# Applying a norm's root behind the matrix products instead of ahead of them, in a fused two-block fp32 kernel

## The chip, the cores and the metric

One core of a Trainium2 chip runs the whole program. The metric is device time in microseconds, the median of three runs. PE is the tensor engine, DVE the vector engine, ACT the scalar engine, POOL the GpSimd engine and SP the queue that loads the weights.

## What is computed

Two transformer blocks on 512 tokens with width 1024, in fp32. The first block (gated linear recurrence, convolution, a PEER layer with 16384 experts) ends in a norm, the second one has an attention with dilated windows, an MLP, a differential attention, an MLP, and a last norm. What matters here is the tail:

```python
def rms_norm(x, g):
    y = x * lax.rsqrt(jnp.mean(x * x, axis=-1, keepdims=True) + EPS)
    return y * g

h = h + g2 * peer_layer(...)
h = rms_norm(h, final_g)                           # norm 2
h = h + attention_a(rms_norm(h, mix_g[0]))         # norm 3
h = h + sq_relu_mlp(rms_norm(h, mlp_g[0]), ...)    # norm 4
h = h + attention_b(rms_norm(h, mix_g[1]))         # norm 5
h = h + sq_relu_mlp(rms_norm(h, mlp_g[1]), ...)    # norm 6
return rms_norm(h, final_g_2)                      # norm 7

def sq_relu_mlp(xn, w_in, w_out):
    h = jax.nn.relu(xn @ w_in)
    return (h * h) @ w_out
```

## The kernel before, in words

The activations stay in SBUF, transposed: hT holds h as eight tiles of 128 features by 512 tokens. Weights come as 568 panels of 128 outputs by 1024 inputs, in one fixed order, through a ring of four slots (SP). A panel is an fp32 product made of three fast ones: the weights are split into a high part (ACT, high_w, line 772) and a low part (POOL, ring_r, line 1874), the activations into a high part (for the norms uT_r, in the MLPs and attention outputs the tiles `parts`) and a low part (sq_r), and PE adds high by high, high by low and low by high, 24 matmuls of 512 columns for a panel (lines 350 to 352). Each panel goes into one of four PSUM banks, and PE may write a bank again when `bank_free` says that it has been read. ACT prepares panel j+3 when panel j is done, so weights are ready two panels ahead.

A norm r runs like this. While the eight panels of the projection before it finish, DVE adds each into hT (`residual`, lines 1593 and 1596), ACT squares the tile into sq (line 792) and PE sums the squares over the partitions with a matmul against ones, two panels later (`behind`, `square_sum`, line 388; an fp32 matmul, which the trace lists as two). After the last panel, `norm` does the last two sums. DVE makes the mean (line 1312), ACT the rough reciprocal root (line 780), DVE one Newton step of three instructions (lines 1305 to 1307). Then DVE scales all eight tiles by weight and root (`scaled`, line 1322), ACT copies their high parts into uT_r (line 820), DVE subtracts to get the low parts in sq_r (line 1334), and only then may PE begin the next panels.

Norm 2's output is itself h (its `scaled` writes hT), and norm 3 squares that again, so these two run one behind the other with no product between them. Norms 3 and 5 feed 24 panels of q, k and v each, which ACT copies out of PSUM (lines 1120, 1122, 1126); the value tiles are then transposed by PE and copied by ACT (line 1114). Norms 4 and 6 feed the MLPs: in groups of eight hidden tiles ACT applies Relu out of PSUM into one of four buffers `gel` (line 1055), DVE squares the tile (line 1673) and splits it (lines 1317, 1318). The order is up(0), then up(g+1), down(g) in turn. All engines meet by semaphores alone; each engine's order is its program text.

## Time and profile before

| | us |
|---|---|
| median of 3 runs (lowest, highest) | 4031.61 (4026.58, 4033.82) |
| the profiled execution's own time | 4038.15 |
| its span, first to last instruction | 4036.3 |
| mean granted TensorE clock | 0.967 of full |
| PE busy | 3796.2 (94%) |
| DVE, ACT, POOL busy | 2159.3, 1339.2, 1370.9 |

Line numbers are those of the kernel before. In the timeline an entry says when an instruction started, how long it ran, and in brackets how long its engine had been idle and who released it. Matmuls overlap, so the distance between starts counts, not their length.

### The profile page before, as it was taken

What the parts mean: (1) busy time and instruction counts of PE and PEld (TensorE: products, weight loads), DVE (VectorE), ACT (ScalarE), POOL (GpSimd) and SP (SyncE); (2) the same over time, 40 slices, a digit from 0 to 9 for tenths busy, and PEclk for the clock granted to TensorE, in tenths of its full rate; (3) what the DMA queues carried; (4) which work ended last, traced back from release to release, by engine and by line L of the source; (5) the groups of instructions that cost most, each with busy time, mean ns of one, the idle gap of its engine ahead of it and who ended that gap; (6) DMA issues with size and microseconds to landing.
All of it is one profiled execution on the core that took longest, in us unless ns stands there. A gap on an engine that the chain in (4) does not pass through costs nothing.

```text
span 4036.3 us, 49951 instructions
## 1 busy us (share of the span) xinstructions
PE 3796.2 (94%) x17036; PEld 2977.2 (74%) x17036; DVE 2159.3 (53%) x3575; ACT 1339.2 (33%) x1852; POOL 1370.9 (34%) x588
## 2 busy tenths in 40 slices
PE   7998997899999999979999999999899989988998
PEld 4888785678888888858888886754588868357886
DVE  3776897507576676237777774125363320546441
ACT  3444322223434344311111112346322233653221
POOL 1122242333343333334444443320144434223442
PEclk8999998999999999989999999989999999999999
DMA  4334321223364554666666652221122222212222
GB/s 171 131 108 147 129 94 53 79 94 110 110 208 136 182 160 158 207 196 183 198 187 182 182 182 86 79 74 46 42 94 95 94 74 96 68 41 82 95 94 78
DMA packets 266639, 486.55 MB, mean 121 GB/s; under 512 B 16721, under 2 KB 148177, under 8 KB 266097
## 3 DMA queue, kind: packets, MB, share of 16 engines
q1 hardware_dynamic: 81936, 299.93, 23.6%
q10 hardware_dynamic: 184580, 184.95, 14.1%
q8 instruction: 81, 1.33, 0.1%
q14 instruction: 42, 0.34, 0.0%
HBM read 415.48 MB, written 84.02 MB: 124 GB/s over the span
## 4 chain that ended last, share of the span: by engine, by line
PE 51%; issue 34%; POOL 11%; DVE 2%; ACT 2%; POOLq 0%; DMA 0%; DVEq 0%; ACTq 0%
PE ps L350 15%; PE ps L352 14%; PE ps L351 14%; POOL ring_r L1874 11%; PE ps L655 3%; PE ps L673 2%; PE ps L663 1%; PE ps L388 1%; DVE sq L1322 1%; ACT arena L1142 0%; PE ps L691 0%; DVE arena L1726 0%; ACT L1177 0%; ACT L1175 0%; ACT high_w L772 0%
## 5 line engine op out<-in xcount | busy, mean ns | idle before, releaser
L1874 POOL TENSOR_TENSOR ring_r<-ring,high_w 128x1024 fp32r<-128x1024 f32 x552 | 1345.1, 2438 | 2495.8 <-ACT high_w L772 1931.5
L350 PE MATMUL ps<-uT_r,high_w 128*128 128x512 f32 x2752 | 1105.4, 402 | 97.5 <-POOL ring_r L1874 40.0
L352 PE MATMUL ps<-uT_r,ring_r 128*128 128x512 f32 x2752 | 1082.3, 393 | 0.0
L772 ACT ACTIVATE high_w<-ring 128x1024 fp32r<-128x1024 f32 x424 | 446.7, 1056 | 1090.7 <-PE ps L352 938.5
L351 PE MATMUL ps<-sq_r,high_w 128*128 128x512 f32 x2048 | 803.5, 392 | 0.0
L351 PE MATMUL ps<-part,high_w 128*128 128x512 f32 x1856 | 735.4, 396 | 0.0
L350 PEld LDWEIGHTS ps<-uT_r,high_w 128*128 128x128 f32 x2752 | 524.7, 191 | 221.3 <-issue 82.8
L350 PE MATMUL ps<-part,high_w 128*128 128x512 f32 x1536 | 613.6, 399 | 4.9 <-POOL ring_r L1874 4.9
L352 PE MATMUL ps<-part,ring_r 128*128 128x512 f32 x1536 | 607.4, 395 | 0.0
L352 PEld LDWEIGHTS ps<-uT_r,ring_r 128*128 128x128 f32 x2752 | 522.9, 190 | 112.1
L351 PEld LDWEIGHTS ps<-sq_r,high_w 128*128 128x128 f32 x2048 | 389.2, 190 | 78.6
L351 PEld LDWEIGHTS ps<-part,high_w 128*128 128x128 f32 x1856 | 350.3, 189 | 89.7 <-issue 7.4
L350 PEld LDWEIGHTS ps<-part,high_w 128*128 128x128 f32 x1536 | 288.9, 188 | 78.2 <-POOL ring_r L1874 5.4
L352 PEld LDWEIGHTS ps<-part,ring_r 128*128 128x128 f32 x1536 | 288.7, 188 | 70.1
L1726 DVE CUSTOM_DVE_ANT_0 arena<-ps,arena 128x512 f32<-128x512 f32 x128 | 87.7, 690 | 392.9 <-PE ps L655 234.8
L1317 DVE TENSOR_SCALAR part<-arena 128x512 fp32r<-128x512 f32 x192 | 292.5, 1523 | 6.6
L1318 DVE TENSOR_TENSOR part<-arena,part 128x512 fp32r<-128x512 f32 x192 | 274.1, 1427 | 6.6
L1596 DVE TENSOR_TENSOR hT<-ps,hT 128x512 f32<-128x512 f32 x80 | 55.4, 692 | 380.4 <-PE ps L352 380.4
L1673 DVE TENSOR_TENSOR arena<-arena 128x512 f32<-128x512 f32 x192 | 134.3, 699 | 226.3 <-ACT arena L1055 117.5
L1000 ACT ACTIVATE act_out<-ps 128x512 f32<-128x512 f32 x128 | 76.5, 598 | 492.1 <-PE ps L352 380.7
L1593 DVE SCALAR_TENSOR_TENSOR hT<-ps,ada,hT 128x512 f32<-128x512 f32 x136 | 102.1, 751 | 234.1 <-PE ps L352 234.1
L1659 DVE TENSOR_TENSOR st<-cst,ps 128x512 f32<-128x512 f32 x128 | 87.6, 684 | 206.2 <-PE ps L582 180.6
(275 smaller groups left out, 4015.1 us busy)
## 6 DMA issues: line engine op xcount, KB each, us to landing
ring<-panels SPq DMA_DIRECT2D x568, 512.0 KB, 3.5
adram<-act_out ACTq DMA_DIRECT2D x128, 256.0 KB, 3.9
gdram<-arena ACTq DMA_DIRECT2D x16, 2048.0 KB, 10.3
arena<-gdram ACTq DMA_DIRECT2D x128, 256.0 KB, 5.4
arena<-adram ACTq DMA_DIRECT2D x128, 256.0 KB, 2.7
arena<-ada_rest ACTq DMA_DIRECT2D x32, 512.0 KB, 4.2
strips_dram<-btab ACTq DMA_DIRECT2D x4, 3584.0 KB
arena<-strips_dram ACTq DMA_DIRECT2D x32, 448.0 KB, 3.3
```

Of the source, the lines that this page charges most:

```text
L350: t_.matmul(out, wh, xh, start=(k == 0), stop=False)
L351: t_.matmul(out, wh, xl, start=False, stop=False)
L352: last = t_.matmul(out, wl, xh, start=False, stop=(k == KT - 1))
L655: t_.matmul(ps[:, qt, :], qs[64 * hh:64 * hh + 64, par, qt * P:(qt + 1) * P], ks[64 * hh:64 * hh + 64, par, :], start=True, stop=True).the ...
L772: s_.activation(high_w[:, j % RING], ring[:, j % RING], ACT.Copy).then_inc(hi_ready, 1)
L1317: S.done(v_.tensor_scalar(high, src, 1.0, None, ALU.mult))
L1318: return v_.tensor_tensor(low, src, high, ALU.subtract)
L1593: ins = v_.scalar_tensor_tensor(out=hT[:, j, :], in0=ps[:, j % BANKS, :], scalar=ada[:, gain + j:gain + j + 1], in1=hT[:, j, :], op0=ALU.m ...
L1659: S.mark(v_.tensor_tensor(arng[:, four, :], keys, of_slots(0), ALU.is_equal))
L1673: S.done(v_.tensor_tensor(gel[:, j % 4, :], gel[:, j % 4, :], other, ALU.mult))
L1726: v_.tensor_tensor_reduce(out=pb[:, par, hh, qt, :], in0=ps[:, qt, :], in1=strip[:, hh, P * (3 - qt):P * (3 - qt) + T], scale=1.0, scalar= ...
L1874: g_.tensor_tensor(ring_r[:, j], ring[:, j], high_w[:, j], ALU.subtract).then_inc(lo_ready, 1)
```

## The change

Norms 3 to 6 no longer scale the activations by the root. The panels run on h times the norm's weight (for norm 3 the product of the weights of norms 2 and 3), which ACT and DVE split tile by tile as each residual tile gets ready (`high_of`, `low_of`), and the root of each token multiplies the panel's result: DVE, not ACT, takes q, k and v out of PSUM and multiplies by rstd; in the MLPs DVE multiplies the relu by rstd before it squares it. PE starts panel 0 and does the last two square sums behind it. Squares go to a ring of three tiles in st instead of sq, with a new semaphore `sq_used`. The two norms that adjoin become one pass: ACT squares both h and h times final_g, PE sums both (banks 4 and 5), and `norms_2_3` makes one root from the other; hT is scaled by norm 2's weight and root while the k panels run. The split attention output moves from uT_r to kT_r (parts[1]), because uT_r is now written while the output projection runs. Norms 0, 1 and 7 stay. The diff, without its smaller pieces:

```diff
             def square_sum(r, k):
-                if k == 0 and r:
+                if k == 0:
                     pe.wait_ge(rs_ms, RS_NORM[r])
-                pe.wait_ge(sq_ready, KT * r + k + 1)
-                ins = t_.matmul(ps[:, 4, :], ones[:], sq[:, k, :], start=(k == 0), stop=(k == KT - 1))
+                if r == 2:
+                    for n in range(2):
+                        pe.wait_ge(sq_ready, KT * r + 2 * k + n + 1)
+                        ins = t_.matmul(ps[:, 4 + n, :], ones[:], st[:, 1 + (2 * k + n) % 3, :], start=(k == 0), stop=(k == KT - 1))
+                        ins.then_inc(stat_done if k == KT - 1 else sq_used, 1)
+                    return
+                pe.wait_ge(sq_ready, KT * (r + (r > 2) - (r > 3)) + k + 1)
+                src = st[:, 1 + k % 3, :] if r in FOLDED else sq[:, k, :]
+                ins = t_.matmul(ps[:, 4, :], ones[:], src, start=(k == 0), stop=(k == KT - 1))
                 if k == KT - 1:
                     ins.then_inc(stat_done, 1)
+                elif r in FOLDED:
+                    ins.then_inc(sq_used, 1)
             def behind(r, j):
                     square_sum(r, j - 2)
             def norm(r):
-                for k in range(0 if r in (0, 3) else KT - 2, KT):
+                for k in range(KT - 2, KT):
...
+            def up(q, r=None):
                 for j in range(8):
-                    panel(q, j, (uT_r, sq_r), ready=None if j else ready)
+                    panel(q, j, (uT_r, sq_r), ready=normed(r) if r and j == 0 else None)
+                    if r and j == 0:
+                        norm(r)
...
-                norm(r)
                 for j in range(16):
                     panel(q_qkv + j // 8, j % 8, (uT_r, sq_r), ready=None if j else normed(r))
+                    if j == 0:
+                        norm(2 if s == 0 else 5)
...
-                    panel(q_wo, j, (uT_r, qT_r), ready=None if j else (a["oT_ready"], 0))
+                    panel(q_wo, j, (kT_r, qT_r), ready=None if j else (a["oT_ready"], 0))
...
+                if r == 2:
+                    for n in range(2):
+                        m = 2 * k + n
+                        if m >= 3:
+                            act.wait_ge(sq_used, m - 2)
+                        s_.activation(st[:, 1 + m % 3, :], hT[:, k, :], ACT.Square, scale=col("final", k) if n else 1.0)\
+                          .then_inc(sq_ready, 1)
+                    return
+                if r in FOLDED and k >= 3:
+                    act.wait_ge(sq_used, FOLDED[r] - 2 + k - 2)
+                s_.activation(st[:, 1 + k % 3, :] if r in FOLDED else sq[:, k, :], hT[:, k, :], ACT.Square).then_inc(sq_ready, 1)
+
+            GAIN = {4: "mlp0", 5: "mix1", 6: "mlp1"}
+
+            def high_of(r, k):
+
+                residual_done(2 if r == 3 else r, k)
+                s_.activation(uT_r[:, k, :], hT[:, k, :], ACT.Copy, scale=small[:, 64 + k:65 + k] if r == 3 else col(GAIN[r], k))\
+                  .then_inc(x_high, 1)
...
+                        if r in (2, 4, 5, 6):
+                            high_of(3 if r == 2 else r, j - 1)
                         square(r, j - 1)
+                if r in (2, 4, 5, 6):
+                    high_of(3 if r == 2 else r, KT - 1)
+                    square(r, KT - 1)
...
+                    if first and j == 1:
+                        root(RS_NORM[4 if s == 1 else 6], 5 if s == 1 else 7)
...
-                    if j < 8:
-                        ins = s_.activation(qT[:, j, :], ps[:, j % BANKS, :], ACT.Copy, scale=-0.125)
...
                     high(q_qkv, j + 3)
+                    if j == 0:
+                        root(RS_NORM[2 if s == 0 else 5], 3 if s == 0 else 6)
+                    if j == 1 and s == 0:
+                        root(RS_NORM[3], 4)
...
+            def low_of(r, k):
+
+                ve.wait_ge(x_high, KT * SPLIT_NORM[r] + k + 1)
+                v_.scalar_tensor_tensor(out=sq_r[:, k, :], in0=hT[:, k, :],
+                                        scalar=small[:, 64 + k:65 + k] if r == 3 else col(GAIN[r], k), in1=uT_r[:, k, :],
+                                        op0=ALU.mult, op1=ALU.subtract).then_inc(u_ready, 1)
+
+            def residuals(q, gain, r=None):
+
+                for j in range(8):
+                    residual(q, j, gain)
+                    if r in FOLDED and j:
+                        low_of(r, j - 1)
+                if r in FOLDED:
+                    low_of(r, 7)
+
+            def norms_2_3():
+
+                ve.wait_ge(stat_done, RS_NORM[3] + 1)
+                rsqrt(RS_NORM[2], D, out=sr)
+                S.done(v_.tensor_tensor(ms[:], sr[:], sr[:], ALU.mult))
+                S.done(v_.scalar_tensor_tensor(out=ms[:], in0=ps[:, 5, :], scalar=1.0 / D, in1=ms[:], op0=ALU.mult, op1=ALU.mult))
+                v_.tensor_scalar(ms[:], ms[:], EPS, None, ALU.add).then_inc(rs_ms, 1)
+                newton(RS_NORM[3])
+                S.done(v_.tensor_tensor(rstd[:], rstd[:], sr[:], ALU.mult))
...
+                if s:
+                    S.done(v_.tensor_tensor(gel[:, j % 4, :], gel[:, j % 4, :], rstd[:], ALU.mult))
                 S.done(v_.tensor_tensor(gel[:, j % 4, :], gel[:, j % 4, :], other, ALU.mult))
...
-                down(s, e + 2)
+                down(s, e + 2, 5 if s == 1 else None)
...
+                if s:
+                    rsqrt(RS_NORM[5], D)
+                for j in range(24):
+                    taken(q_qkv, j)
+                    bank = ps[:, j % BANKS, :]
+                    if j < 8:
+                        ins = v_.scalar_tensor_tensor(out=qT[:, j, :], in0=bank, scalar=-0.125, in1=rstd[:], op0=ALU.mult, op1=ALU.mult)
+                    elif j < 16:
+                        ins = v_.tensor_tensor(kT[:, j - 8, :], bank, rstd[:], ALU.mult)
+                    else:
+                        if j >= 18:
+                            ve.wait_ge(vt_done, 8 * s + j - 17)
+                        ins = v_.tensor_tensor(vf[:, j % 2, :], bank, rstd[:], ALU.mult)
+                    ins.then_inc(bank_free[j % BANKS], 1)
+                    if s == 0 and j == 7:
+                        for k in range(KT):
+                            S.mark(v_.scalar_tensor_tensor(out=hT[:, k, :], in0=hT[:, k, :], scalar=col("final", k), in1=sr[:],
+                                                           op0=ALU.mult, op1=ALU.mult))
+                        S.wait()
...
-            for j in range(KT):
-                residual(Q_WO_A, j)
-            norm(4, lambda k: col("mlp0", k))
+            attention(0, Q_QKV_A)
+            residuals(Q_WO_A, None, 4)
+            rsqrt(RS_NORM[4], D)
             hidden(1, Q_MLP_A, 4)
```

## Rows read from the trace of the kernel before

**Rows 1.** The page: instruction count and busy time of each engine.

```profile
span 4036.3 us, 49951 instructions
PE 3796.2 (94%) x17036; PEld 2977.2 (74%) x17036; DVE 2159.3 (53%) x3575; ACT 1339.2 (33%) x1852; POOL 1370.9 (34%) x588
```

**Rows 2.** Waits of PE from 2505 us on (engine, line, releaser: total, times, longest).

```profile
PE ps L350 <- DVE sq_r L1334: 39.3, 4, 9.9
PE ps L388 <- ACT sq L792: 9.4, 6, 5.3
PE ps L691 <- issue: 5.0, 1, 5.0
```

**Rows 3.** Timeline, norms 2 and 3 (start us, length, engine line; [idle before <-releaser]).

```profile
2504.73 0.75 DVE L1593 SCALAR_TENSOR_TENSOR hT<-ps,ada,hT 128x512 f32<-128x512 f32 x1 [5.70 <-PE ps L352]
2512.00 5.39 DVE L1322 SCALAR_TENSOR_TENSOR hT<-hT,cc,st 128x512 f32<-128x512 f32 x8
2523.61 0.69 DVE L1312 TENSOR_SCALAR st<-ps 128x512 f32<-128x512 f32 x1 [6.21 <-PE ps L388]
2524.39 0.63 ACT L780 ACTIVATE st<-st 128x512 f32<-128x512 f32 x1 [6.24 <-DVE st L1312]
2525.05 0.69 DVE L1305 SCALAR_TENSOR_TENSOR st<-st 128x512 f32<-128x512 f32 x1 [0.76 <-ACT st L780]
2527.24 5.39 DVE L1322 SCALAR_TENSOR_TENSOR sq<-hT,cc,st 128x512 f32<-128x512 f32 x8
2532.54 4.90 DVE L1334 TENSOR_TENSOR sq_r<-sq,uT_r 128x512 fp32r<-128x512 f32 x8
2540.57 0.60 ACT L1120 ACTIVATE arena<-ps 128x512 f32<-128x512 f32 x1 [7.28 <-PE ps L352]
```

**Rows 4.** Four stretches, last panel's end to next panel's end (us; busy; clock; DMA).

```profile
2504.73:2540.57 35.84, 19.94 (x47) 10.55 (x46) 21.89 (x33) 14.98 (x25) 2.35 (x1) 0.76 0.05 15
2910.02:2931.76 21.74, 11.13 (x31) 7.38 (x30) 13.66 (x21) 9.25 (x14) 2.35 (x1) 0.76 0.08 26
3283.84:3307.04 23.20, 11.61 (x31) 7.42 (x30) 14.19 (x23) 10.73 (x16) 2.35 (x1) 0.71 0.07 23
3644.27:3665.83 21.56, 10.95 (x31) 7.25 (x30) 13.66 (x21) 9.25 (x15) 2.35 (x1) 0.76 0.08 24
```

**Rows 5.** Timeline of ACT in the first up-projections after norm 4.

```profile
2931.76 0.60 ACT L1055 ACTIVATE arena<-ps 128x512 f32<-128x512 f32 x1 [8.41 <-PE ps L352]
2937.20 0.60 ACT L1055 ACTIVATE arena<-ps 128x512 f32<-128x512 f32 x1 [3.89 <-PE ps L352]
```

**Rows 6.** Timeline of DVE in two output projections: panel ends without and with a square sum.

```profile
3600.79 0.69 DVE L1596 TENSOR_TENSOR hT<-ps,hT 128x512 f32<-128x512 f32 x1 [3.05 <-PE ps L352]
3606.39 0.69 DVE L1596 TENSOR_TENSOR hT<-ps,hT 128x512 f32<-128x512 f32 x1 [4.91 <-PE ps L352]
...
2903.57 0.69 DVE L1596 TENSOR_TENSOR hT<-ps,hT 128x512 f32<-128x512 f32 x1 [5.76 <-PE ps L352]
2910.02 0.69 DVE L1596 TENSOR_TENSOR hT<-ps,hT 128x512 f32<-128x512 f32 x1 [5.76 <-PE ps L352]
```

**Rows 7.** Timeline of DVE and POOL in one hidden tile of the first MLP.

```profile
2937.83 0.69 DVE L1673 TENSOR_TENSOR arena<-arena 128x512 f32<-128x512 f32 x1 [1.49 <-ACT arena L1055]
2938.56 0.43 DVE L1317 TENSOR_SCALAR part<-arena 128x512 fp32r<-128x512 f32 x1
2938.83 2.41 POOL L1874 TENSOR_TENSOR ring_r<-ring,high_w 128x1024 fp32r<-128x1024 f32 x1 [3.03 <-ACT high_w L772]
2939.02 2.76 DVE L1318 TENSOR_TENSOR part<-arena,part 128x512 fp32r<-128x512 f32 x1
```

**Rows 8.** Timeline of ACT and POOL where the qkv panels of the second attention end.

```profile
3435.04 0.60 ACT L1126 ACTIVATE arena<-ps 128x512 f32<-128x512 f32 x1 [3.89 <-PE ps L352]
3435.54 1.05 ACT L772 ACTIVATE high_w<-ring 128x1024 fp32r<-128x1024 f32 x1
3436.66 2.34 POOL L1874 TENSOR_TENSOR ring_r<-ring,high_w 128x1024 fp32r<-128x1024 f32 x1 [3.53 <-ACT high_w L772]
```

More of the change, by code:

```diff
@@ L70 @@
 SPLIT_NORM = {0: 0, 1: 1, 3: 2, 4: 3, 5: 4, 6: 5}
+FOLDED = {3: 0, 4: 16, 5: 23, 6: 30}
 class Steps:
@@ L233, in build @@
         qT, kT = (view(4096 * n, KT, T) for n in range(2))
-        qT_r = parts[0]
+        qT_r, kT_r = parts[:2]
         vtok = view(8192, TT, D)
@@ L604, in hidden @@
             def hidden(s, q8, groups):
-                up(q8, normed(4 if s == 1 else 6))
+                up(q8, 4 if s == 1 else 6)
                 with pe.Fori(0, groups // 2 - 1) as i:
@@ L800, in last_before @@
                     if j:
+                        if r in (2, 4, 5, 6):
+                            high_of(3 if r == 2 else r, j - 1)
                         square(r, j - 1)
+                if r in (2, 4, 5, 6):
+                    high_of(3 if r == 2 else r, KT - 1)
+                    square(r, KT - 1)
             def norm(r):
-                for k in range(0 if r in (0, 3) else KT - 1, KT):
+                for k in range(0 if r == 0 else KT - 1, KT):
                     square(r, k)
                 root(RS_NORM[r], r + (r >= 1))
-                if r in SPLIT_NORM and r:
+                if r == 1:
                     high_x(r)
@@ L1105, in _ @@
             last_before(2, Q_PEER + 31)
-            norm(2)
             def attention(s, r, q_qkv):
                 a = att[s]
-                norm(r)
                 def token_major(j):
@@ L1181, in high_b @@
                     act.wait_ge(b_out, u + 1)
-                    s_.activation(uT_r[:, u, :], act_out[:, 0, :], ACT.Copy).then_inc(b_high, 1)
+                    s_.activation(kT_r[:, u, :], act_out[:, 0, :], ACT.Copy).then_inc(b_high, 1)
                 def round_b(n):
@@ L1259, in attention @@
                         act.wait_ge(weighed, k + 1)
-                        s_.activation(uT_r[:, k, :], qT[:, k, :], ACT.Copy).then_inc(o_high, 1)
+                        s_.activation(kT_r[:, k, :], qT[:, k, :], ACT.Copy).then_inc(o_high, 1)
                 else:
@@ L1273, in _ @@
             last_before(4, Q_WO_A)
-            norm(4)
             hidden(1, Q_MLP_A, 4)
@@ L1280, in _ @@
             last_before(6, Q_WO_B)
-            norm(6)
             hidden(2, Q_MLP_B, 4)
@@ L1320, in scaled @@
             def scaled(r, k, gain):
-                v_.scalar_tensor_tensor(out=(hT if r == 2 else sq)[:, k, :], in0=hT[:, k, :], scalar=gain(k),
+                v_.scalar_tensor_tensor(out=sq[:, k, :], in0=hT[:, k, :], scalar=gain(k),
                                         in1=rstd[:], op0=ALU.mult, op1=ALU.mult).then_inc(upre if r in SPLIT_NORM else u_ready, 1)
@@ L1366, in gain_of @@
             def gain_of(r):
+                if r == 1:
+                    S.done(v_.tensor_tensor(small[:, 64:72], cc[:, COLS["final"]:COLS["final"] + 8], cc[:, COLS["mix0"]:COLS["mix0"] + 8],
+                                            ALU.mult))
                 name = "norm1" if r == 0 else "norm2"
@@ L1679, in up, with down @@
                     tile(s, g, j, par)
-            def down(s, q):
-                for j in range(8):
-                    residual(q, j, 40 if s == 0 else None)
+            def down(s, q, r=None):
+                residuals(q, 40 if s == 0 else None, r)
             def hidden(s, q8, groups):
                 up(s, q8, 0, 0)
-                with S.loop(groups // 2 - 1, 32) as i:
+                with S.loop(groups // 2 - 1, 48 if s else 32) as i:
                     up(s, i * 4 + (q8 + 1), i * 2 + 1, 1)
@@ L1709, in _, with attention @@
                 stored_down(i * 2 + (q + 2), i * 2 + 2, 0)
-            down(0, q + GROUPS - 1)
-            norm(2, lambda k: col("final", k))
-            def attention(s, r):
+            down(0, q + GROUPS - 1, 3)
+            norms_2_3()
+            def attention(s, q_qkv):
                 a = att[s]
-                norm(r, lambda k: col("mix0" if s == 0 else "mix1", k))
+                if s:
[7 more added lines that the diff above has]
+                        ins = v_.tensor_tensor(kT[:, j - 8, :], bank, rstd[:], ALU.mult)
+                    else:
+                        if j >= 18:
[7 more added lines that the diff above has]
+                        S.wait()
                 def strip_wait(n, hh):
@@ L1849, in _ @@
             S.done(v_.tensor_scalar(lamc[:, 3:4], lamc[:, 2:3], -LAMBDA_INIT, None, ALU.add))
-            attention(1, 5)
-            for j in range(KT):
-                residual(Q_WO_B, j)
-            norm(6, lambda k: col("mlp1", k))
+            attention(1, Q_QKV_B)
+            residuals(Q_WO_B, None, 6)
+            rsqrt(RS_NORM[6], D)
             hidden(2, Q_MLP_B, 4)
@@ L1908, in low_b @@
                 po.wait_ge(b_high, u + 1)
-                g_.tensor_tensor(qT_r[:, u, :], act_out[:, 0, :], uT_r[:, u, :], ALU.subtract).then_inc(a["oT_ready"], 1)
+                g_.tensor_tensor(qT_r[:, u, :], act_out[:, 0, :], kT_r[:, u, :], ALU.subtract).then_inc(a["oT_ready"], 1)
             at_b = 8 * (Q_WO_B - Q_HEADS) // RING
```

59 lines of the change are left out of this document (20 added, 39 removed).

## The prediction, made before the changed kernel ran

> **What bounds the kernel now.** I read the page first: PE is busy 94% of the span, DVE 53%, ACT 33%, POOL 34% [rows 1]. So time is gained only where PE stands still, or where it does work that can be left out. Next I asked for the waits of PE from 2505 us on, the part that the change touches. The largest is four waits, 39.3 us together, of the first matmul of a panel for the low part of the activations; then 9.4 us in six waits of the square sums for ACT [rows 2]. Everything else listed there belongs to attention and is 5 us or less. The four are norms 3, 4, 5 and 6. The timeline of the first shows the chain: the last residual tile at 2504.73, eight scalings to hT from 2512.00, the second mean at 2523.61, eight more scalings, eight subtractions, and only at 2540.57 is the first new panel out of PE [rows 3]. That wait is listed as 9.9 us at most, because the square sums in the middle cut it, so the list of waits understates what a norm costs. The right measure is from the end of the last old panel to the end of the first new one. Those four stretches are 35.84, 21.74, 23.20 and 21.56 us, 102.34 us in sum, with the granted clock at 0.76, 0.76, 0.71 and 0.76 of full [rows 4]. Part of the time PE had the lower of its two levels, 1.2 instead of 2.4 GHz, so that the first panel behind the standstill is slow as well; that is inside these lengths.
>
> **What the stretches become.** A panel on (uT_r, sq_r) that waits for nothing takes 5.44 us (2937.20 less 2931.76) [rows 5]. One square sum costs PE 0.85 us: panels of an output projection end 5.60 us apart without one and 6.45 us with one [rows 6].
>
> Norms 4, 5 and 6. After the last old panel come the sum of tile 5 (0.85), panel 0 (5.44), then the sums of tiles 6 and 7, which now lie behind panel 0 (1.70). Together 7.99 us each, 24.0 us for three. They take 66.50 us now. Saved: 42.5 us.
>
> Norms 2 and 3. Each tile has two sums. After the last panel: two sums of tile 5 (1.70), panel 0 (5.44), four sums (3.40), 10.5 us. The five tiles summed behind earlier panels get one more each, 4.25 us. 14.8 us in place of 35.84. Saved: 21.0 us. The count is the same 16 sums as before: eight of them stood in the gap and now stand between panels, and can't be hidden. That is why the double norm gives less than its length promises.
>
> Sum 63.5 us. One sum might wait: the last square of norm 2/3 needs a slot of the ring of three, freed by the first of the four sums. That is 0.85 us after panel 0 ends; the square takes about 0.6, and PE has two more sums (1.7 us) before it asks for it. Nothing.
>
> **Is the new work hidden?** (a) Low parts at panel 0. Count from the end T of the last panel. ACT does high_w (1.05 us [rows 8]), then high part 6, square 6 and high part 7 at up to 0.60 us each, the length of its copies in rows 5: done by T+2.8. The timeline has DVE's subtraction, with both inputs in SBUF, take 2.76 us where it meets POOL's 2.41 us weight subtraction, though POOL began 0.19 us before it; the same form without POOL takes about 0.6 (eight in 4.90) [rows 3, 7]. It ended 0.54 us after POOL did. So DVE's low parts 6 and 7 may be held until POOL ends at about T+3.6, and be done at T+4.2 and T+4.8. Panel 0 starts at about T+0.7, asks for tile 6 after 18 of its 24 matmuls (T+4.8) and for tile 7 three later (T+5.5). It just fits: cost zero, bound above 0.7 us for each of four norms if either is one instruction later.
>
> (b) The root must exist when PE wants bank 0 again, at panel 4 (qkv), 3 x 5.44 = 16.3 us after the sums end. For norm 5: mean, ACT's root, three Newton instructions and one read, about 5 us. For norms 2/3 the chain is twice that: two means, two roots, six Newton instructions, a square, a product, an addition of EPS and a last product, at 0.72 us from one Newton step to the next (2525.05 to the scaling at 2527.24 are three) and 0.63 us per root [rows 3] about 10.5 us. The second root also stands in ACT behind taken(1) and a high_w, at about 6.6 us after the sums. So first read at 11.1 us, with 5.2 us to spare. In the MLPs the reader is ACT's relu, which does not need the root at all; four buffers `gel` give another four panels. Cost zero.
>
> (c) The extra product in the MLPs, 64 of 0.69 us, 44 us of DVE. Before, a tile takes 4.0 us from the relu (2937.83 to 2941.78) out of 5.44 [rows 7]. After: products until 1.4 us, then the copy of the high part meets POOL instead of the subtraction, is released at about 3.4, and the tile ends at about 4.5. Below 5.44, so PE stays the bound. When DVE is late at the start of an MLP (by some 5 us, the root), it must catch up: it needs 2.6 us of each 5.44, and POOL leaves it 3.0.
>
> (d) q, k, v out of PSUM by DVE: 48 times 0.69 instead of ACT's 0.60, on an engine that sat idle there. The eight scalings of hT (5.4 us) lie behind k panels with four banks between. Zero. ACT now begins the last high_w 0.5 us earlier (3435.04 instead of 3435.54), and POOL, which stages the second attention only after its last subtraction, follows [rows 8]; PE waits for both, in the first attention for ACT. I take 0.9 us off for the two, less 0.2 for DVE's slower copy.
>
> (e) The output projection reads kT_r instead of uT_r: the trace has two pitches for a panel without sums, 5.44 and 5.60 us [rows 5, 6], and these 16 panels already have the longer one. The tile's place might decide which, so the bounds are 16 x 0.16 = 2.6 us less or as much more; I take zero.
>
> The sum is 64.2 us, against the profiled execution's own 4038.15 us: 3973.9. The median of the runs is 4031.61, 6.5 lower, so I take the same gain from it: 3967.4 us.
>
> A rule that speaks against this change is in the Trainium skill, SBUF — State Buffer, "The single rule": DVE instructions with two SBUF inputs and GpSimd instructions that read SBUF lock each other out whole. By that rule the low parts, the Newton steps and the product by the root can all be held, which the trace shows for the subtraction alone. In norms 2/3 it holds two steps of the chain for up to 2.4 us each; first read would come at 15.9 instead of 11.1 us, still ahead of 16.3, so by it the sum stays at 3967.4.
>
> **The rivals.** *Part of the gap stays.* The margins of (a) are half a microsecond and of (b), all holds counted, half a microsecond too. If low parts are late in every norm at one POOL length (2.4 us) and the double chain overshoots by 3, 12.6 us are lost: 3980. For it: DVE is held for a whole POOL instruction in every hidden tile. Against: the margins as counted include that hold. Chance 0.2.
>
> *DVE becomes the bound of the up-projections (slower).* Place: `tile`, once the four `gel` buffers are used up. It decides from 5.44 us a tile. If both the new product and the copy or subtraction were held for a whole POOL instruction, a tile would take 4.0 + 2.77 = 6.7 us; 64 x 1.3 = 83 us, more than the 64 gained, so some 4050. Against it: POOL runs one 2.41 us instruction per panel and can't hold DVE twice in one, and down panels leave time to catch up. Chance 0.02.
>
> *The gaps were not what ends last.* If PE, freed of them, waited for weights instead (ACT and POOL must keep the pace through the norm), the time would be 4031. Against: in all panels away from norms ACT waits 3.9 us per panel for PE [rows 5], so they have room. Chance 0.02.
>
> *More than counted,* some 6 us more (3961): attention starts earlier in other ways, fewer holds. Chance 0.06.
>
> **How the numbers follow.** The forecast has 0.70, its own spread some 5 us either way (the runs of before spread by 7). The range goes from 3958, for the rival that gains more, to 3984, for the gap that stays in part. A measurement of this kernel can tell about 0.2%, 8 us, from no change; both of the main cases are far beyond that: faster 0.96, same 0.02, slower 0.02.
>
> **What would show it.** The wait of L350 for the low parts in norms 3 to 6 (39.3 us) falls to under 2. The four stretches become 10 to 11 us and three times 8, at full clock. PE busy hardly changes; DVE's rises by 44 us from the products and 33 from the PSUM reads, less the 32 scalings left out. PE shows no wait on ACT's relu or DVE's tile in the MLPs, and none for bank 0 at the fifth q panel. I am wrong if a wait for the new PSUM read appears there, if panel 0 stops at its seventh tile, or if up panels come more than 5.5 us apart.

## The result, and the profile after

The changed kernel takes 3968.36 us (median of 4 runs, 3962.99 to 3969.05), the kernel before 4030.86 beside it (4026.58 to 4033.82). The ratio is 0.9843, 95% interval 0.9826 to 0.986: faster by 1.57%, 62.5 us. The forecast was 3967.4, in a range of 3958 to 3984. Run once more with later experiments, the changed kernel came to 3961.81 and the same ratio, 0.9842 (0.9826 to 0.9859).

The profiled executions are 4038.15 us before and 3962.99 after, which is 75.2 apart. Segment by segment, below, 61.5 us of that can be put down to a cause or a place that repeats; the rest lies where executions of one kernel differ as well.

First the page after, instructions and busy time of each engine, to be held against [rows 1]:

```profile
span 3961.2 us, 50054 instructions
PE 3769.2 (95%) x17036; PEld 2968.6 (75%) x17036; DVE 2267.1 (57%) x3659; ACT 1315.1 (33%) x1804; POOL 1388.0 (35%) x588
```

PE has the same 17036 matmuls. DVE is up by 107.8 us and 84 instructions, ACT down by 24.1 us and 48 instructions, PE down by 27.0 us. The waits of PE from 2500 us on (engine, line, releaser: total, times, longest) answer to [rows 2]:

```profile
PE ps L675 <- ACT arena L1176: 6.4, 7, 1.7
PE ps L703 <- issue: 4.8, 1, 4.8
PE ps L351 <- DVE part L1900: 3.8, 4, 2.3
PE ps L351 <- POOL part L1979: 3.5, 1, 3.5
```

The 39.3 us for `sq_r` are gone from the list, and so are the 9.4 us for squares. What leads it now all belongs to attention. L351 waits there for the low part of the heads' output, as before.

The timeline of DVE from the last residual of the peer layer on, with lines left out, answers to [rows 3]:

```profile
2501.12 0.75 DVE L1646 SCALAR_TENSOR_TENSOR hT<-ps,ada,hT 128x512 f32<-128x512 f32 x1 [3.20 <-PE ps L353]
2502.82 3.04 DVE L1364 SCALAR_TENSOR_TENSOR sq_r<-hT,small,uT_r 128x512 fp32r<-128x512 f32 x2 [0.95 <-ACT uT_r L819]
2511.76 0.69 DVE L1338 TENSOR_SCALAR st<-ps 128x512 f32<-128x512 f32 x1 [5.90 <-PE ps L391]
...
2519.07 2.24 DVE L1331 SCALAR_TENSOR_TENSOR st<-st 128x512 f32<-128x512 f32 x1 [1.80 <-ACT st L790]
...
2523.53 1.89 DVE L1775 SCALAR_TENSOR_TENSOR arena<-ps,st 128x512 f32<-128x512 f32 x3
```

The last residual is followed at once by the two low parts, together 3.04 us, over at T+4.74. The first of them took 2.38 us instead of 0.75 beside GpSimd's weight subtraction (below, "held" is short for this). The double root is made beside panels 1 to 3. Its first use is at 2523.53, where three finished panels lie waiting, so three reads run back to back.

Three windows after (start:end length, PE, PEld, DVE, ACT, POOL busy, clock, DMA share and GB/s): the double norm, from the last residual up to the last of its sums; norm 4, up to the end of panel 0; the first MLP from last residual to last residual. The first two stand where [rows 4] had 35.84 and 21.74 us:

```profile
2501.12:2511.79 10.67, 10.67 (x37) 6.79 (x36) 3.81 (x4) 6.52 (x9) 3.25 (x2) 1.00 0.31 100
2881.14:2887.50 6.36, 6.36 (x27) 4.88 (x26) 3.74 (x3) 3.33 (x6) 2.41 (x1) 1.00 0.26 84
2881.14:3241.34 360.20, 360.20 (x1553) 291.32 (x1552) 186.76 (x172) 94.59 (x116) 162.23 (x64) 1.00 0.28 94
```

In all of them PE is busy the whole length, at full clock. The stretch of norm 4 is a standstill no more. The same MLP before, also from last residual to last residual:

```profile
2910.02:3283.84 373.82, 363.21 (x1553) 293.10 (x1552) 159.40 (x148) 94.74 (x116) 153.78 (x64) 0.99 0.28 90
```

The same 1553 matmuls took 363.21 us of PE; they now take 360.20. So of the 13.6 us gained, 10.6 was standing still and 3.0 was matmuls at the lower clock behind the standstill.

Divided at last residuals and at the reads of the last v panels, the whole second half compares as follows (us; each boundary is the start of an instruction in the timeline; before, the last v panels are read at 2668.58 and, as in [rows 8], at 3435.04):

| segment | before | after | difference | forecast |
|---|---|---|---|---|
| last peer residual to last v panel (norms 2 and 3) | 163.85 | 138.68 | -25.17 | -25.3 |
| attention A | 198.08 | 197.90 | -0.2 | -0.7 in both together |
| output projection A | 43.36 | 43.44 | +0.1 | 0 |
| MLP A (norm 4) | 373.82 | 360.20 | -13.62 | -13.75 |
| to last v panel (norm 5) | 151.20 | 136.15 | -15.05 | -15.21 |
| attention B | 165.75 | 160.15 | -5.6 | |
| output projection B | 43.48 | 44.94 | +1.5 | 0 |
| MLP B (norm 6) | 373.64 | 360.20 | -13.44 | -13.57 |
| tail (norm 7) | 18.4 | 18.4 | 0 | 0 |

The forecast of the first segment is 35.84 less 10.54; the 4.25 us for sums behind earlier panels lie ahead of that boundary. Of the 75.2 us, the four norm segments are 67.3. Less those 4.25 and the 1.5 of output projection B, 61.5 us are left, and the medians are 62.5 apart. The profiled executions of the changed kernel and its variants show what is chance in the rest: where they don't change an MLP or the tail they repeat it to 0.1 us, but attention A took between 190.2 and 197.9 us, attention B between 160.1 and 166.8, and the last peer residual came between 2499 and 2512 us in kernels with the same front. The traces of the changed kernel and of the one before have the granted clock at 0.91 in attention A, 0.96 in attention B of the changed kernel and 0.97 ahead of 2500 us. The 5.6 us of attention B, and the part ahead of 2500 us (3.6 us shorter though it holds 4.25 more), are within that spread, so nothing is read from them.

### The profile page after: what moved, and what is told of

The parts are those of the page before. It is cut to its first block, busy times and chain, and to the rows that moved or that the text cites. A ratio compares the mean times of both kernels' runs of the same rounds, so it can differ in the third digit from the quotient of the medians.

```text
span 3961.2 us, 50054 instructions
## 1 busy us (share of the span) xinstructions
PE 3769.2 (95%) x17036; PEld 2968.6 (75%) x17036; DVE 2267.1 (57%) x3659; ACT 1315.1 (33%) x1804; POOL 1388.0 (35%) x588
## 4 chain that ended last, share of the span: by engine, by line
PE 51%; issue 35%; POOL 11%; ACT 1%; DVE 1%; POOLq 0%; DMA 0%; DVEq 0%; ACTq 0%
PE ps L351 15%; PE ps L353 15%; PE ps L352 15%; POOL ring_r L1944 11%; PE ps L667 3%; PE ps L685 2%; PE ps L675 1%; PE ps L396 1%; PE ps L391 0%; ACT arena L1170 0%; DVE arena L1798 0%; PE ps L703 0%; ACT L1205 0%; ACT L1203 0%; POOLq L1943 0%
## 5 line engine op out<-in xcount | busy, mean ns | idle before, releaser
L351 PE MATMUL ps<-uT_r,high_w 128*128 128x512 f32 x2624 | 1046.9, 399 | 49.8 <-POOL ring_r L1944 38.5
L353 PE MATMUL ps<-uT_r,ring_r 128*128 128x512 f32 x2624 | 1027.1, 391 | 0.0
L352 PE MATMUL ps<-part,high_w 128*128 128x512 f32 x1856 | 735.3, 396 | 0.0
L351 PE MATMUL ps<-part,high_w 128*128 128x512 f32 x1664 | 669.5, 402 | 12.1 <-POOL ring_r L1944 4.8
L353 PE MATMUL ps<-part,ring_r 128*128 128x512 f32 x1664 | 658.6, 396 | 0.0
L351 PEld LDWEIGHTS ps<-uT_r,high_w 128*128 128x128 f32 x2624 | 496.9, 189 | 161.0 <-issue 36.8
L353 PEld LDWEIGHTS ps<-uT_r,ring_r 128*128 128x128 f32 x2624 | 495.7, 189 | 105.1
L1343 DVE TENSOR_SCALAR part<-arena 128x512 fp32r<-128x512 f32 x192 | 419.4, 2185 | 6.6
L352 PEld LDWEIGHTS ps<-part,high_w 128*128 128x128 f32 x1856 | 351.2, 189 | 88.6 <-issue 7.4
L351 PEld LDWEIGHTS ps<-part,high_w 128*128 128x128 f32 x1664 | 314.1, 189 | 94.2 <-issue 8.4
L353 PEld LDWEIGHTS ps<-part,ring_r 128*128 128x128 f32 x1664 | 314.3, 189 | 74.5
L352 PE MATMUL ps<-part_x,high_w 128*128 128x512 f32 x448 | 177.4, 396 | 0.0
```

The costliest lines, as they stand in the source:

```text
L351: t_.matmul(out, wh, xh, start=(k == 0), stop=False)
L352: t_.matmul(out, wh, xl, start=False, stop=False)
L353: last = t_.matmul(out, wl, xh, start=False, stop=(k == KT - 1))
L1343: S.done(v_.tensor_scalar(high, src, 1.0, None, ALU.mult))
```

## The experiments

**The last sums ahead of panel 0 or behind it.** The change puts the last two square sums (four in the double norm) behind the first new panel. Here they stand ahead of it again; all else is folded.

```diff
+                    if r and j == 0:
+                        norm(r)
                     panel(q, j, (uT_r, sq_r), ready=normed(r) if r and j == 0 else None)
-                    if r and j == 0:
-                        norm(r)
```

The same is done in attention.

> The changed kernel, but PE does the last two square sums (tiles 6 and 7) of norms 3 to 6 ahead of panel 0 instead of behind it. Theory (PE's order matters, the squares are not ready when the last panel ends): square 7 is written about 3.4 us after the last panel, so panel 0 starts some 1.8 us later in norms 4, 5, 6 and 0.9 us later in norms 2/3; in sum about 6 us slower than the changed kernel, and a wait of PE for ACT's squares of 5 to 7 us comes back. Rival (the order is indifferent, because PE would wait for the low parts at panel 0 anyway): within 1.5 us of the changed kernel.

Measured: 3969.92 us, ratio to before 0.9862 (0.9846 to 0.9879). The time alone doesn't settle it, but the segments do: 0.80 for the double norm and 1.88 each for norms 4, 5 and 6, 6.4 us in all, where about 6 was expected. PE's waits for squares are back with 4.3 us in three of them; 5 to 7 was expected. Nearly all of the gain is therefore the fold itself; the order of the sums is a tenth of it.

**What a square sum costs.** Each sum of the double norm is done a second time, into a bank that nobody reads.

```diff
                         pe.wait_ge(sq_ready, KT * r + 2 * k + n + 1)
+                        t_.matmul(ps[:, 6 + n, :], ones[:], st[:, 1 + (2 * k + n) % 3, :], start=(k == 0), stop=(k == KT - 1))
                         ins = t_.matmul(ps[:, 4 + n, :], ones[:], st[:, 1 + (2 * k + n) % 3, :], start=(k == 0), stop=(k == KT - 1))
```

> The changed kernel with each of the 16 square sums of norms 2/3 done twice (the copy goes to a bank that nobody reads). Theory (square sums between panels lie bare on PE, 0.85 us each): 13.6 us slower. Rival (PE has slack there, or only the four behind panel 0 count): 0 to 3.4 us slower.

Measured: 3977.18 us, ratio 0.9881 (0.9864 to 0.9897). The medians, 8.8 us apart from different sets of runs, can't settle 13.6; the segments can. The six extra sums behind the last residual make the first segment 143.82 instead of 138.68: 5.14, or 0.857 each. The down panels ahead of it come 9.02 us apart instead of 7.30, five times 1.72. That is 13.7 us in all. Each sum lies wholly on the path, on either side of the last panel.

**How full VectorE is.** A product like the new one is done once more, and in another kernel three times more, in each hidden tile of both MLPs; nobody reads it. The edit with one:

```diff
                 if s:
+                    for _ in range(1):
+                        S.done(v_.tensor_tensor(act_out[:, 0, :], gel[:, j % 4, :], rstd[:], ALU.mult))
                     S.done(v_.tensor_tensor(gel[:, j % 4, :], gel[:, j % 4, :], rstd[:], ALU.mult))
```

> The changed kernel with one more DVE product in each of the 64 hidden tiles, written to an unused buffer. Theory (PE is the bound, DVE's tile may be longer than a panel for a while because four buffers and the down panels absorb it): a tile then takes 5.8 us against 5.44 us a panel, lag of some 11 us after 16 tiles, no stall: within 2 us. Rival (the extra product has put DVE at the edge): 64 times 0.36 to 0.7 us, 23 to 45 us slower.

> The changed kernel with three more DVE products in each hidden tile. DVE needs about 7.2 us a tile with POOL's subtraction holding it once. Theory (only the first 16 tiles in a row can run DVE out of buffers): 10 to 30 us slower in all, PE waiting near the end of the second up group of each MLP and at the start of the first down group. Rival (DVE bound from the first tile on): 64 times 1.8, 115 us slower.

One more costs nothing: 3967.12 us, ratio 0.9852 (0.9835 to 0.9869), both MLPs 360.20 as without it. Three more cost 25.5 and 26.0 us in the MLPs, and 4017.15 in all (0.9972, 0.9962 to 0.9983), which gives back most of the gain. Between 10 and 30 was expected, and the two MLPs alone are 51.5: the price of running out of buffers was set too low, though the place was right. The windows of the first MLP with one more, and then of a stretch of three in the kernel with three more:

```profile
2886.01:3246.21 360.20, 360.20 (x1553) 291.35 (x1552) 211.36 (x204) 94.69 (x115) 164.65 (x64) 1.00 0.28 94
```

```profile
2985.00:3000.04 15.04, 0.86 (x4) 0.40 (x3) 14.49 (x21) 1.06 (x1) 2.34 (x1) 0.68 0.10 35
3000.04:3005.04 5.00, 5.00 (x14) 3.97 (x15) 1.65 (x3) 0.00 (x0) 0.00 (x0) 0.61 0.01 3
3005.04:3015.00 9.96, 9.96 (x45) 8.07 (x44) 1.38 (x2) 2.12 (x2) 2.99 (x2) 1.00 0.21 61
```

The stall has its place: not in the up panels, which have four banks and four `gel` tiles, but behind them. VectorE still works on tiles when the first down panels are finished, their residuals come late, and PE wants their banks (wait of 14.19 us for `hT`, DVE busy 14.49 of 15.04 us). Then PE runs at a clock of 0.61 for some 5 us. The three waits for `hT` in that MLP are 14.19, 2.08 and 2.08, 18.4 us, and two for the weights' low part add 1.4. The rest of its 25.5 is PE's busy time, 365.95 us for the same 1553 matmuls instead of 360.20.

**One fold alone.** Norm 4 is put back as before (sums in one go, scale, high part, low part, no root in the tiles of MLP A). The other three stay folded.

```diff
-FOLDED = {3: 0, 4: 16, 5: 23, 6: 30}
+FOLDED = {3: 0, 5: 16, 6: 23}
...
-            rsqrt(RS_NORM[4], D)
+            norm(4, lambda k: col("mlp0", k))
...
-                if s:
+                if s == 2:
                     S.done(v_.tensor_tensor(gel[:, j % 4, :], gel[:, j % 4, :], rstd[:], ALU.mult))
```

> Norm 4, between the first output projection and the first MLP, is put back as it was: sums in one go ahead of the products, h scaled by the root and the weight, then split, and no root in that MLP's tiles. The other three stay folded. Theory (each fold is worth its own gap and nothing else moves): the first MLP from last residual to last residual goes from 360.20 back to 373.82, the second stays at 360.20, the norms 2 and 3 gap stays at 10.7; whole time 13.6 us above the changed kernel. Rival (the folds gain from each other, by the clock or by the weight transfers that a gap let run ahead): the difference is under 9 or over 18 us, or another segment moves by over 1 us.

Measured: 3978.76 us against 3961.81 of the changed kernel on the same chip; ratios to before 0.9881 (0.9865 to 0.9896) and 0.9842. The difference of medians, 17.0 us, is blurred by attention. MLP A takes 372.67, MLP B stays at 360.20 and the first segment at 138.67: the fold is worth 12.5 us, and no other segment outside attention moves by over 0.4 us. That is 1.1 less than expected, since this gap came out shorter than before's, 20.59 us to the relu of panel 0 instead of 21.74; why is open. The wait is back alone, in the list of waits of this kernel, and its window has the low clock, 0.75 where [rows 4] has 0.76:

```profile
PE ps L351 <- DVE sq_r L1359: 9.8, 1, 9.8
```

```profile
2877.93:2898.52 20.59, 9.98 (x31) 6.54 (x30) 13.66 (x21) 9.26 (x14) 2.35 (x1) 0.75 0.08 27
```

**How much room the double root has.** Ten products that nobody reads are put into its chain, each waited for.

```diff
                 rsqrt(RS_NORM[2], D, out=sr)
+                for _ in range(10):
+                    S.done(v_.tensor_tensor(act_out[:, 0, :], sr[:], sr[:], ALU.mult))
```

> Ten more products of 128x512 stand in the chain of the roots of norms 2 and 3, each waited for, which nobody reads. By the theory the chain is off the path with slack: its first read of a panel comes 12.2 us after the last residual's sums and the bank is needed at 15.9, so 3.7 us are free. At 0.69 to 0.72 us each the ten are 7.0 us: the first attention segment (last residual of the peer layer to last v panel) grows by 3.3 us, 138.7 to 142, more if some are held by GpSimd at 2.4 (each hold adds 1.7), and nothing else moves: +3 to +7 in all. Rival (the chain is on the path already, its whole length counts): +7 or more with no hold. Second rival (later work has slack that takes it all up): +0.

Measured: 3976.37 us, ratio 0.9871 (0.9856 to 0.9886). The first segment is 147.92, 9.2 us longer, and none of the others outside attention changes by over 0.1 us. 3.3 was expected without holds, and 3 to 7 with them. 9.2 is outside that and inside the bounds of the first rival, which says 7 or more if the whole chain is on the path; so the time alone doesn't decide, and the timeline has to. In the medians it is 14.6 us (3961.81 to 3976.37), with attention's spread in it. Lines of the timelines of DVE and PE in this kernel:

```profile
2519.06 0.69 DVE L1338 TENSOR_SCALAR st<-ps 128x512 f32<-128x512 f32 x1 [5.89 <-PE ps L391]
...
2522.69 9.30 DVE L1382 TENSOR_TENSOR act_out<-st 128x512 f32<-128x512 f32 x10
...
2536.11 2.72 DVE L1333 SCALAR_TENSOR_TENSOR st<-st 128x512 f32<-128x512 f32 x1
2538.86 2.71 DVE L1387 TENSOR_TENSOR st<-st 128x512 f32<-128x512 f32 x1
2541.60 2.49 DVE L1777 SCALAR_TENSOR_TENSOR arena<-ps,st 128x512 f32<-128x512 f32 x4
```

```profile
2542.44 0.77 PE L351 MATMUL ps<-uT_r,high_w 128*128 128x512 f32 x1 [7.08 <-DVE arena L1777]
```

From the start of the first mean to the first read are 22.54 us here and 11.77 without the ten, so the chain became 10.8 longer, not 7.0. The ten took 9.30 us rather than about 7.2, because one of them was held (2.77), and two later steps were held at 2.7; without the ten only one step was (2.24). PE waits 7.08. The room is thus 10.8 less 7.1, 3.7 us, as stated: had the whole chain been on the path, as the rival has it, PE would have waited all of the 10.8. The other 2 us are PE's own: nine matmuls behind the wait begin 0.43 us apart instead of 0.23, at the lower clock. So the theory of the room holds, and the price of overstepping it was set too low.

**The sums on VectorE.** The second experiment says that a square sum on PE is never hidden, the third that VectorE has room. So VectorE adds up the squares (one copy, seven additions), and PE keeps one product with ones per mean, behind panel 0. ScalarE makes high part and square ahead of its next weight part.

```diff
+            def add_square(r, k):
...
+                    src = st[:, 1 + m % 3, :]
+                    if k:
+                        ve.wait_ge(sq_used, used + m - two + 1)
+                        ins = v_.tensor_tensor(acc[n], acc[n], src, ALU.add)
+                    else:
+                        ins = v_.tensor_scalar(acc[n], src, 1.0, None, ALU.mult)
+                    ins.then_inc(acc_ready if k == KT - 1 else sq_used, 1)
...
             def norm(r):
+                if r in ADDED:
+                    pe.wait_ge(rs_ms, RS_NORM[r])
+                    for n in range(2 if r == 2 else 1):
+                        pe.wait_ge(acc_ready, ADDED[r] + n)
+                        t_.matmul(ps[:, 4 + n, :], ones[:], acc[n], start=True, stop=True).then_inc(stat_done, 1)
+                    return
```

In the first of the three kernels, for norms 4, 5 and 6, VectorE adds into bank 5 of PSUM while the product reads an SBUF tile that it doesn't fill, so three roots aren't the reference's. In the other two both are the same SBUF tile, with the same instructions and waits; the additions there have both inputs in SBUF, in the first only one. DVE at norm 4 in the first:

```profile
L1408 DVE TENSOR_TENSOR ps<-ps,st 128x512 f32<-128x512 f32 x7 | 4.9, 694 | 0.1
L1410 DVE TENSOR_SCALAR ps<-st 128x512 f32<-128x512 f32 x1 | 0.7, 689 | 0.0
```

With them the changed kernel ran once more.

> The changed kernel itself once more, beside the three others, so that they can be compared with it on one chip. Both theories: 3968, 1.6% under the kernel before. Segments without attention in them to repeat within 0.1 us (an MLP from last residual to last residual 360.20), those with attention by up to 6 us with the clock. Open question it is to answer: whether the output projection of the second block takes 44.9 us again (before: 43.48), or whether that was chance.

> For norms 4, 5 and 6 VectorE adds up the eight squares itself as they come (one copy, seven additions of 128x512), and TensorE has one product with ones at the end instead of eight, behind panel 0; ScalarE does the high part and the square of a tile ahead of the next weight part. By the theory TensorE is the bound there and each of the seven products at 0.85 us is on the path: each norm gives 6.0 us, 18 in all, 3968 to 3950, with an MLP from last residual to last residual at 354.2, since VectorE has room: a residual, a low part and an addition are 0.75 + 0.75 + 0.72 us in a panel of 5.4 to 5.6, up to 5.6 where GpSimd holds two of them. Rival (VectorE is that full: the holds push the residuals past the panels, or the last addition comes too late for the sum behind panel 0): under 9 us of gain, or slower, with a TensorE wait for the last sum or for a residual.

> As sums_on_vector, with the running sums in SBUF tiles of their own, and for the double norm 2 and 3 too (two running sums, so two copies and fourteen additions of 128x512 on VectorE, two products with ones left of sixteen). By the theory each product with ones that goes is 0.85 us of TensorE's path: 18 us for norms 4, 5 and 6 as in sums_on_vector (segments 39.0, 354.2, 134.4, 39.2 and 358.5), 14 x 0.857 = 12.0 for the double one (its down panels before the last residual 7.28 us apart become 5.6), so 30 us: 3962 to 3932, 2.4% under the kernel before. Rival (VectorE's own time decides where it adds two tiles of SBUF: a held one is 2.4 to 2.7 us instead of 0.7, and the double norm gives it a residual, a low part and two additions in a panel of 5.6, 2.9 us free of holds, 6.3 with two held, over 8 with three): the double norm gains under 6 us and the down panels show a TensorE wait for a residual, or the three others fall back from 354.2 towards 360.

> As sums_on_vector_4, and norms 1 and 7 (not folded, with their squares kept in a tile of eight) get the running sum on VectorE too. By the theory seven more products in each leave TensorE's path, 2 x 6.0 us: 3932 to 3920, with the last MLP from last residual to last residual at 353 instead of 358.5, and the tail behind the last residual within 1 us of 18.4 (one product fewer, one addition more). Rival (the tail now waits for square, addition and product one behind the other, and norm 1's split waits likewise): each of the two gives under 3 us, the tail grows by over 1.5 us.

| us | output proj. A | MLP A | to last v panel B | MLP B | tail | whole time | ratio to before |
|---|---|---|---|---|---|---|---|
| changed kernel, with the first of these | 43.39 | 360.20 | 136.13 | 360.18 | 18.4 | 3961.81 | 0.9842 (0.9826 to 0.9859) |
| norms 4, 5, 6, in PSUM | 39.04 | 354.20 | 134.38 | 358.46 | 18.4 | 3949.47 | 0.9797 (0.9782 to 0.9812) |
| double norm, 4, 5, 6 | 39.04 | 354.22 | 134.37 | 358.44 | 18.4 | 3939.64 | 0.9779 (0.9757 to 0.9801) |
| norms 1 to 7 | 39.04 | 354.25 | 134.39 | 354.32 | 19.1 | 3924.03 | 0.975 (0.9726 to 0.9773) |

The question to the changed kernel is answered: output projection B takes 45.32 us again, so its length was not the chance of one execution. The theory of the sums holds segment by segment. Norms 4 and 6 give 4.4 us ahead of the last residual and 1.7 behind it, norm 5 likewise 4.3 and 1.8. The down panels ahead of the double norm come 5.58 us apart, not 7.30, and the segment behind it is 135.21, not 138.68. Norm 7 gives 4.1 in the MLP and takes 0.7 back in the tail, where PE now waits 2.4 us for the last addition. For norm 1 the last five panels ahead of the last residual end 5.54 us apart instead of 6.45.

What the rival feared, additions held by GpSimd, came up only in the third kernel, in norms 1 and 7, where ScalarE keeps its old order. Six of norm 1's seven additions are held there and three of norm 7's, and the panels still come 5.54 and 5.60 us apart, as without a sum. DVE at norm 7:

```profile
3876.39 2.48 DVE L1387 TENSOR_TENSOR act_out<-act_out,sq 128x512 f32<-128x512 f32 x1 [0.85 <-ACT sq L820]
3880.45 0.69 DVE L1695 TENSOR_TENSOR hT<-ps,hT 128x512 f32<-128x512 f32 x1 [1.58 <-PE ps L355]
3881.99 2.48 DVE L1387 TENSOR_TENSOR act_out<-act_out,sq 128x512 f32<-128x512 f32 x1 [0.85 <-ACT sq L820]
3886.05 0.69 DVE L1695 TENSOR_TENSOR hT<-ps,hT 128x512 f32<-128x512 f32 x1 [1.57 <-PE ps L355]
```

In the double norm and norms 4 to 6 no addition is held. Nor is any of the 32 low parts, of which 28 were held in the changed kernel. DVE's low parts in the changed kernel, then its additions and low parts in the second of the three (x count | busy us, mean ns of one | idle before):

```profile
L1364 DVE SCALAR_TENSOR_TENSOR sq_r<-hT,cc,uT_r 128x512 fp32r<-128x512 f32 x24 | 52.0, 2176 | 21.3 <-ACT uT_r L819 21.3
L1364 DVE SCALAR_TENSOR_TENSOR sq_r<-hT,small,uT_r 128x512 fp32r<-128x512 f32 x8 | 17.4, 2179 | 6.7 <-ACT uT_r L819 6.7
```

```profile
L1403 DVE TENSOR_TENSOR act_out<-act_out,st 128x512 f32<-128x512 f32 x28 | 19.2, 686 | 0.3
L1378 DVE SCALAR_TENSOR_TENSOR sq_r<-hT,cc,uT_r 128x512 fp32r<-128x512 f32 x24 | 18.0, 752 | 1.4
L1378 DVE SCALAR_TENSOR_TENSOR sq_r<-hT,small,uT_r 128x512 fp32r<-128x512 f32 x8 | 6.0, 751 | 0.1
```

The second edit in these kernels goes with it: ScalarE makes the high part and the square ahead of the weight part that starts GpSimd, and VectorE begins its last instruction of a panel before GpSimd starts (2861.15 and 2862.00 us at norm 4's last panel but one). So one held addition per panel costs nothing (norms 1 and 7), and the low part and additions cost nothing in the new order of ScalarE; low part and additions in the old order were not run, nor was the new order alone. The timeline of DVE at norm 4 in the second kernel of the three, and its first MLP:

```profile
2865.30 0.69 DVE L1695 TENSOR_TENSOR hT<-ps,hT 128x512 f32<-128x512 f32 x1 [3.47 <-PE ps L355]
2866.06 1.48 DVE L1378 SCALAR_TENSOR_TENSOR sq_r<-hT,cc,uT_r 128x512 fp32r<-128x512 f32 x2
2867.46 1.48 DVE L1403 TENSOR_TENSOR act_out<-act_out,st 128x512 f32<-128x512 f32 x2
2871.63 0.69 DVE L1352 TENSOR_SCALAR st<-ps 128x512 f32<-128x512 f32 x1 [2.69 <-PE ps L414]
```

```profile
2865.30:3219.52 354.22, 354.22 (x1539) 288.68 (x1538) 180.06 (x180) 94.97 (x115) 162.78 (x64) 1.00 0.28 95
```

1539 matmuls instead of 1553: seven sums fewer, each listed as two matmuls (two behind the residual for norm 4, five ahead of the last one for norm 5), 5.98 us. PE is busy throughout, as in the same MLP of the changed kernel, so the time that went is that of the products and not of a wait. The whole time falls short of the sum of the parts in the first kernel (12.3 us under the changed kernel, where 18 was expected), by some 8 us in the second (3939.64 for an expected 3932) and 4 in the third, no more than attention varies between runs. The last kernel computes what the reference asks and beats both: 2.5% under before, about 1% under the change.

## Why the prediction was right

**The measure.** The list of waits shows 39.3 us, and the stretches from panel to panel 102.3. The stretches were the right base: the gain of the norm segments is 67.3 us, well over the 48.7 of the two waits of [rows 2].

**The term of norms 4 to 6** (7.99 us left of each, 42.5 gained): 13.62, 15.05 and 13.44 measured, 42.1 in sum. The sum of tile 5, panel 0, two more sums and panel 1 were put at 13.43 us and took 6.36 and 7.20, 13.56. With norm 4 alone unfolded its fold is worth 12.5 and the other segments stay, so norm 4 is independent of the others to within about 1 us; norms 5 and 6 were not unfolded alone.

**The double norm** (21.0 gained): 25.17 less the 4.25 that went ahead of the boundary, 20.9. The extra sums at 0.85 each are confirmed with 0.857.

**(a) The low parts** were to be done at T+4.2 and T+4.8, held by GpSimd; the second was done at T+4.74, and PE shows no wait for them. The prediction priced the holds only here, at the last two. In the trace 28 of all 32 low parts were held, 69.4 us in all where the 32 subtractions before took 19.6. This is the larger part of why DVE's busy time rose by 107.8 us and not by the 55 that the prediction's signs add up to (44 and 33, less some 22 for the scalings). It cost nothing, since PE shows no wait for a low part, but it was not foreseen. PE's busy time, which was to hardly change, fell by 27.0 us, 0.7%; 3.0 and 2.8 of that, in the two MLPs, are matmuls that no longer run at the lower clock behind a standstill.

**(b) The double root** was to be first read 11.1 us after the sums; it was 11.8 from the start of the first mean, with one step held, and the room was measured at 3.7, not 5.2. The first read must thus start by about 15.5 us and not 16.3, since the bank comes free only when it has been read. By that, the prediction's bound of 15.9 with two steps held for up to 2.4 us each would not have fitted; in the changed kernel the one hold made its step 1.55 us longer. That the term is zero is shown; that it would stay zero with two full holds is not.

**(c) The hidden tile** was put at 4.5 us. It takes 4.7 in the tile shown, with the copy of the high part held in the place of the subtraction of [rows 7]:

```profile
2906.21 0.69 DVE L1727 TENSOR_TENSOR arena<-arena,st 128x512 f32<-128x512 f32 x1 [0.76 <-ACT arena L1090]
2906.94 0.69 DVE L1728 TENSOR_TENSOR arena<-arena 128x512 f32<-128x512 f32 x1
2907.67 2.50 DVE L1343 TENSOR_SCALAR part<-arena 128x512 fp32r<-128x512 f32 x1
2910.21 0.69 DVE L1344 TENSOR_TENSOR part<-arena,part 128x512 fp32r<-128x512 f32 x1
```

That 0.7 us of a panel's 5.44 is free is shown by the one product more. The rival of VectorE as the bound is real, with its point between one and three further products, and its place at the residuals behind the up panels and not in `tile` where I had it.

**(d)** The 0.7 us at the start of attention can't be seen under its spread: attention A is 0.2 us shorter, B 5.6 where repeats differ by more. **(e)** Output projection A keeps its pitch: 43.36 and 43.44. Projection B is 1.5 us longer, and 1.4 to 1.8 in all runs of the changed kernel and of its variants with the sums on PE. It does the same work as projection A. A window of the changed kernel at its start shows twelve matmuls in 4 us at a clock of 0.57, where before had 18 at full clock:

```profile
3537.64:3541.64 4.00, 4.00 (x12) 3.09 (x11) 0.69 (x1) 1.06 (x1) 2.36 (x1) 0.57 0.42 135
```

PE had waited 3.5 us for GpSimd ahead of it, as in the kernel before. What decides whether the low clock falls there I did not find; in the first kernel with sums on VectorE, with the same attention, the projection ran at full clock and took 39.20 rather than the 40.6 of the other two. This part of the result the steps don't cover, and it stays open.

**Luck.** The steps add up to 63.0 us of the 63.5 forecast, and that is not luck. That the median came within 1 us of 3967.4 is: the same kernel's medians were 3968.36 and 3961.81, and the 1.5 us lost in projection B and the 0.7 expected in attention lie inside that difference.

## What to carry to other kernels

Measure a barrier between two phases from the last old tile to the first new one: the list of waits showed 48.7 us here where 67 were gained, and leaves out the matmuls at the lower clock behind the standstill. A scale that is the same for all rows of a product can be applied behind it, if its chain fits beside the tiles whose buffers are already there; find that room by lengthening the chain until the next engine waits. Once the barrier is gone, look again at what stood in it: the square sums, which nothing hid, were worth another 1% on an engine with room. Where GpSimd holds VectorE up, look at what starts GpSimd: with ScalarE's weight part put behind its high part and square, none of 32 low parts was held instead of 28.

## What the runs showed of the hardware

- A standstill of PE costs more than its length. Behind a wait of 7.08 us nine matmuls started 0.43 us apart instead of 0.23, 2 us on top; behind one of 14.19 us the granted clock was 0.61 over 5 us. By the PE busy time of the same MLP, the norm before had 3.0 us of it.
- Not only the subtraction of two SBUF tiles in [rows 7] is held. Beside GpSimd's weight subtraction a product took 2.71 us, Newton steps 2.24 and 2.72, the low part 2.38 (0.75 without GpSimd), and the copy of the high part, which has one SBUF input, 2.50 us instead of 0.43. That the one with a single input is held as well agrees with the Trainium skill, SBUF — State Buffer, "Who interferes with whom": a VectorE instruction in a 2-port mode, which `tensor_scalar` can enter, contends with GpSimd for the shared port pair too, and whichever issues first has it for the whole instruction. No run here shows which mode the copy was in.
- It works both ways. GpSimd's weight subtraction takes 2.41 us in the tiles before [rows 7] and 2.68 after, where it begins inside one of VectorE's products:

```profile
2907.20 2.68 POOL L1944 TENSOR_TENSOR ring_r<-ring,high_w 128x1024 fp32r<-128x1024 f32 x1 [2.76 <-ACT high_w L782]
```
